# A transposed triangular inverse taken by VectorE in 32x32 blocks, and norm sums kept as columns and spread by TensorE

## The reference

```
def chunk_gated_delta(q, k, v, g, beta, s0):
    ...
    lmat = jnp.where(strict, jnp.einsum('nbhid,nbhjd->nbhij', k_beta, kb) * decay, 0.0)
    rhs = jnp.concatenate([vb * bb[..., None], k_beta * jnp.exp(gc)[..., None]], axis=-1)
    sol = lax.linalg.triangular_solve(lmat + jnp.eye(c, dtype=F32), rhs, left_side=True,
                                      lower=True, unit_diagonal=True)
    u, w = sol[..., :dv], sol[..., dv:]
    ...

def gated_deltanet(h, conv_buf, s0, w_qkv, w_conv, w_ab, dt_bias, a_log, w_g, o_norm_g, w_out):
    ...
    o, s_new = chunk_gated_delta(q, k, v, g, beta, s0)
    gate = jax.nn.silu(h @ w_g).reshape(bsz, t, GDN_HEADS, GDN_DV)
    o = rmsnorm(o, o_norm_g) * gate
    return o.reshape(bsz, t, GDN_HEADS * GDN_DV) @ w_out, new_buf, s_new
```

## Time and profile before

| | us |
|---|---|
| median of 3 runs | 1561.23 (1558.59 to 1562.16) |
| the profiled execution, its own time | 1560.17 |
| its span, first to last instruction | 1558.4 |
| heads, from 1113 to 1285 of the span | 172 |

### The profile page before, as it was taken

One profiled execution on the slowest core, in us unless ns is written; L12 is line 12 of the kernel. 1 busy time (PEld: TensorE's weight loads), 2 busy tenths in 40 slices (PEclk: granted clock), 3 DMA queues, 4 the chain that ended last, 5 costly groups with the idle time before them and its releaser, 6 DMA issues.

```text
span 1558.4 us, 32581 instructions
## 1 busy us (share of the span) xinstructions
PE 1524.9 (98%) x10378; PEld 1486.8 (95%) x10378; DVE 803.6 (52%) x1791; ACT 734.4 (47%) x1406; POOL 1082.0 (69%) x1040
## 2 busy tenths in 40 slices
PE   9999999999999999999999999999899999999998
PEld 8999999998999999888999999999888889999997
DVE  4555554017555313996555521666668766555401
ACT  6654444445444435566544433557544424444432
POOL 5568887764777678986777767766645656767674
PEclk9999999999999999999999999999999999999999
DMA  6344444552444655322656445544411215444453
GB/s 238 122 131 150 157 148 152 149 147 93 152 159 140 164 148 160 101 63 87 168 152 166 138 137 142 192 129 141 129 60 66 83 69 183 150 158 141 125 151 111
DMA packets 88110, 212.49 MB, mean 136 GB/s; under 512 B 25600, under 2 KB 33312, under 8 KB 88032
## 3 DMA queue, kind: packets, MB, share of 16 engines
q1 hardware_dynamic: 88032, 211.49, 44.1%
HBM read 201.80 MB, written 9.66 MB: 136 GB/s over the span
## 4 chain that ended last, share of the span: by engine, by line
PE 92%; DVE 4%; issue 1%; ACT 1%; POOL 1%; DMA 1%; DVEq 0%; SPq 0%; POOLq 0%; ACTq 0%
PE bank L887 26%; PE bank L889 26%; PE bank L888 26%; PE bank L1125 2%; PE bank L1264 2%; PE bank L1286 1%; PE bank L1275 1%; PE bank L1324 1%; PE bank L1178 1%; DMA fst<-in_d_st 1%; POOL M L715 0%; DVE bank L2247 0%; PE bank L1354 0%; PE bank L1306 0%; DVE ssq L1939 0%
## 5 line engine op out<-in xcount | busy, mean ns | idle before, releaser
L609 POOL TENSOR_TENSOR wlo<-raw,whi 128x512 fp32r<-128x512 f32 (+3 forms) x398 | 458.0, 1151 | 378.8 <-ACT whi L1417 341.2
L887 PE MATMUL bank<-Gh,whi 128*128 128x320 f32 x1912 | 597.3, 312 | 3.1 <-DVE M L2229 1.9
L889 PE MATMUL bank<-Gh,wlo 128*128 128x320 f32 x1912 | 591.9, 310 | 0.0
L888 PE MATMUL bank<-Gl,whi 128*128 128x320 f32 x1912 | 591.8, 310 | 0.0
L611 POOL TENSOR_TENSOR wlo<-raw,whi 128x512 fp32r<-128x512 f32 (+3 forms) x398 | 478.6, 1203 | 0.0
L1417 ACT ACTIVATE whi<-raw 128x1024 fp32r<-128x1024 f32 (+3 forms) x400 | 374.8, 954 | 53.2 <-PE bank L889 38.9
L887 PEld LDWEIGHTS bank<-Gh,whi 128*128 128x128 f32 x1912 | 360.0, 188 | 5.4 <-DVE M L2229 2.2
L888 PEld LDWEIGHTS bank<-Gl,whi 128*128 128x128 f32 x1912 | 359.9, 188 | 1.1
L889 PEld LDWEIGHTS bank<-Gh,wlo 128*128 128x128 f32 x1912 | 359.8, 188 | 0.0
L887 PE MATMUL bank<-Hh,whi 128*128 128x320 f32 x912 | 283.9, 311 | 4.0 <-DVE Hl L2188 2.5
L889 PE MATMUL bank<-Hh,wlo 128*128 128x320 f32 x912 | 282.2, 309 | 0.0
(11 more groups left out here) (388 smaller groups left out, 1844.9 us busy)
## 6 DMA issues: line engine op xcount, KB each, us to landing
raw<-in_f_up SPq DMA_DIRECT2D x176, 512.0 KB, 3.4
raw<-in_f_down SPq DMA_DIRECT2D x64, 384.0 KB, 3.2
raw<-in_f_down SPq DMA_DIRECT2D x64, 320.0 KB, 3.2
raw<-in_c_pw SPq DMA_DIRECT2D x24, 512.0 KB, 3.7
raw<-in_a_in SPq DMA_DIRECT2D x16, 512.0 KB, 3.9
raw<-in_d_qk SPq DMA_DIRECT2D x16, 512.0 KB, 3.6
raw<-in_d_vg SPq DMA_DIRECT2D x16, 512.0 KB, 3.6
raw<-in_a_out SPq DMA_DIRECT2D x8, 512.0 KB, 3.5
```

The source lines that it names most:

```text
L609: pool.tensor_tensor(wlo[k][:, 0:half], raw[k][:, 0:half], whi[k][:, 0:half].bitcast(F32), ALU.subtract).then_inc(half_ready, 1)
L887: nc.tensor.matmul(dst, wh, h, start=start and n == 0, stop=False)
L888: nc.tensor.matmul(dst, wh, lo, start=False, stop=False)
L889: ins = nc.tensor.matmul(dst, wl, h, start=False, stop=stop and end and n == len(tiles) - 1)
```

## The change

The third product of levels 0 to 3 goes. Up to there the inverse has no entry outside diagonal blocks of 32, so DVE transposes `Tm` into `TT` in blocks of 32x32. Level 4 keeps its product under a new name. The sum of squares becomes three columns (tokens along the partitions): `sq` is the weight of the product and one column of ones is what moves. ACT takes the root of 3 columns, DVE inverts the 6 of both heads at once, and PE spreads them over the partitions with a product of the broadcast column and the identity; `head_scale` reads the result in PSUM. In pairs 1 to 3 this is done within levels 2 and 3 of the inverse (for the pair before), for the last pair behind the first unit of `d_out`.

```
 def gdn_pair(b):                                  # PE
-    def change_turned(lev, x):
-        ...
-        for c in range(3 if lev < 2 else 2):
+    def last_change_turned(x):
+        pe.wait_ge(b_ready, b * 10 + (9 + x))
+        pe.wait_ge(inv_ready, b * 10 + (7 + x))
+        pe.wait_ge(kv_scaled, b * 2 + (x + 1))
+        for c in range(2):
             ins = nc.tensor.matmul(T(bank[4 * x + 2], c), T(Bm[x], c), T(TT[x], c), start=True, stop=True)
         ins.then_inc(tb_done, 1)
     for lev in range(5):
-        below(lev, 0)
-        if lev > 0:
-            change_turned(lev - 1, 1)
-        below(lev, 1)
-        if lev < 4:
-            change(lev, 0)
-        change_turned(lev, 0)
-        if lev < 4:
-            change(lev, 1)
-    change_turned(4, 1)
+        for x in range(2):
+            below(lev, x)
+        if lev in (2, 3) and not isinstance(b, int):
+            pe.wait_ge(rinv_ready, b * 1)
+            pe.wait_ge(qt_ready, b * 2 + (lev - 1))
+            spread(lev - 2, bank[4 * (lev - 2) + 1])
+        for x in range(2):
+            if lev < 4:
+                change(lev, x)
+            else:
+                last_change_turned(x)
...
+                        if not isinstance(b, int):
+                            pe.wait_ge(h_mid, b * 2 + (htile(3, False) + x - 1))
                         nc.tensor.matmul(T(bb, 0), T(TT[x], 0), T(vp[x], 0), start=True, stop=True).then_inc(u_done, 1)
...
-                        nc.tensor.matmul(bank[4 * x + 2][:, 0:NT], ones[:, :], sq[x][:, 0:NT], start=True, stop=True)\
-                            .then_inc(osum_done, 1)
+                        for i, (first, _, _) in enumerate(TOKENS):
+                            ins = nc.tensor.matmul(bank[4 * x + 2][:, TW + i:TW + i + 1], sq[x][:, first:first + P], ones[:, 0:1],
+                                                   start=True, stop=True)
+                        ins.then_inc(osum_done, 1)
...
+def spread(x, dst):                               # PE
+    for i, (first, a, z) in enumerate(TOKENS):
+        ins = nc.tensor.matmul(dst[:, a:z], rinv[x][:, i:i + 1].to_broadcast([P, P]),
+                               ident[:, a - first:z - first], start=True, stop=True)
+    ins.then_inc(spread_done, 1)
...
                 for m in range(4):                # PE, d_out
                     pe.wait_ge(ss_ready, 7 + m // 2)
                     unit(u0 + m, m, Hh, Hl, d_out_banks[m][:, 0:NT], range(6), ready=(h_ready, h0), end=False)
+                    if m == 0:
+                        pe.wait_ge(rinv_ready, 4)
+                        for x in range(2):
+                            pe.wait_ge(s_ready, 31 + x)
+                            spread(x, bank[4 * x + 2])
...
-                        nc.scalar.activation(sq[x][:, 0:NT], bank[4 * x + 2][:, 0:NT], ACT.Sqrt, scale=1.0 / P,
+                        nc.scalar.activation(rinv[x], bank[4 * x + 2][:, TW:TW + 3], ACT.Sqrt, scale=1.0 / P,
...
-def head_invert(h, x, i):                         # DVE
-    dve.wait_ge(osd_ready, h + (x + 1))
-    q = sq[x][:, NT // 4 * i:NT // 4 * (i + 1)]
-    S.mark(vec.reciprocal(q, q))
+def head_inverse(n):
+    dve.wait_ge(osd_ready, n)
+    vec.reciprocal(dc[:, 2:8], dc[:, 2:8]).then_inc(rinv_ready, 1)
...
 for lev in range(5):                              # DVE
-    for x in range(2):
-        if lev < 4:
-            ... Tm[x] -= bank[4 * x + 3]
-        if later and x == 1 and lev < 4:
-            head_invert(b * 2 - 2, lev // 2, 2 * (lev % 2))
-        ... TT[x] -= bank[4 * x + 2]
-    if later and 2 <= lev < 4:
-        head_invert(b * 2 - 2, lev - 2, 1)
+    if lev < 4:
+        for x in range(2):
+            ... Tm[x] -= bank[4 * x + 3]
+        for x in range(2):
+            dve.wait_ge(tm_ready, b * 8 + (2 * lev + x + 1))
+            vec.transpose(TT[x][:, 0:w], Tm[x][:, 0:w]).then_inc(inv_ready, 1)
+    else:
+        ... TT[x] -= bank[4 * x + 2]                for both x
+    if later and lev in (2, 3):
+        head_scale(b * 2 - 2, lev - 2, bank[4 * (lev - 2) + 1])
...
                         if c == 0 and later:
-                            head_invert(b * 2 - 2, 0, 3)
-                            head_invert(b * 2 - 2, 1, 3)
-                            head_scale(b * 2 - 2, 0)
-                            head_scale(b * 2 - 2, 1)
```

More of the change, by code:

```diff
@@ L373, in trunk_kernel @@
         scr_n = nc.dram_tensor("scr_n", [2 * HEADS, NT], F32).ap()
+        rinv = [dc[:, 2 + 3 * x:5 + 3 * x] for x in range(2)]
+        TOKENS = ((0, 0, P), (P, P, 2 * P), (NT - P, 2 * P, NT))
         GDN_STORED = 18 + 1 + 2 * HEADS
@@ L391, in trunk_kernel @@
         LN_READY, GT_READY, SQRT_READY, RW_READY_A, COLS_READY = 3, 4, 7, 9, 10
-        PAIR_STEPS = 14
+        PAIR_STEPS = 6
         block = ctx.enter_context(nc.Block())
@@ L672, in scaled_keys @@
                     if not (isinstance(b, int) and b == 0):
[L673 removed]
+                        pool.wait_ge(tb_done, b * 2 + (x - 1))
                     pool.wait_ge(k_ready, b * 2 + (x + 1))
@@ L1389, in _ @@
                     if m >= 6:
-                        pe.wait_ge(osd_ready, 7)
                         pe.wait_ge(og_ready, 7)
+                        pe.wait_ge(h_mid, h0 + 7)
                     unit(u0 + m, m % 4, Hh, Hl, d_out_banks[m][:, 0:NT], range(KT))
@@ L2421, in differences, with head_scale @@
                     ins.then_inc(diff_ready if dst is dec else diffi_ready, 1)
-                def head_invert(h, x, i):
-                    dve.wait_ge(osd_ready, h + (x + 1))
-                    q = sq[x][:, NT // 4 * i:NT // 4 * (i + 1)]
-                    S.mark(vec.reciprocal(q, q))
-                def head_scale(h, x):
-                    S.wait()
+                def head_inverse(n):
+                    dve.wait_ge(osd_ready, n)
+                    vec.reciprocal(dc[:, 2:8], dc[:, 2:8]).then_inc(rinv_ready, 1)
+                def head_scale(h, x, src):
+                    dve.wait_ge(spread_done, h + (x + 1))
                     dve.wait_ge(og_ready, h + (x + 1))
-                    vec.tensor_tensor(hbuf[x][:, :], hbuf[x][:, :], sq[x][:, 0:NT], ALU.mult).then_inc(h_mid, 1)
+                    vec.tensor_tensor(hbuf[x][:, :], hbuf[x][:, :], src[:, 0:NT], ALU.mult).then_inc(h_mid, 1)
                 S.wait()
@@ L2465, in gdn_pair @@
                                 S.mark(ins)
+                    if later:
+                        head_inverse(b * 2)
                     for lev in range(5):
                         w = (3 if lev < 2 else 2) * P
-                        for x in range(2):
-                            if lev < 4:
+                        if lev < 4:
+                            for x in range(2):
                                 dve.wait_ge(bt_done, b * 8 + (2 * lev + x + 1))
@@ L2472, in gdn_pair @@
                                     .then_inc(tm_ready, 1)
[L2473 to L2479 removed]
+                            for x in range(2):
+                                dve.wait_ge(tm_ready, b * 8 + (2 * lev + x + 1))
+                                vec.transpose(TT[x][:, 0:w], Tm[x][:, 0:w]).then_inc(inv_ready, 1)
+                        else:
+                            for x in range(2):
+                                dve.wait_ge(tb_done, b * 2 + (x + 1))
+                                vec.tensor_tensor(TT[x][:, 0:w], TT[x][:, 0:w], bank[4 * x + 2][:, 0:w], ALU.subtract)\
+                                    .then_inc(inv_ready, 1)
+                        if later and lev in (2, 3):
+                            head_scale(b * 2 - 2, lev - 2, bank[4 * (lev - 2) + 1])
                         if lev == 4 and not last:
@@ L2509, in gdn_pair @@
                                                          op0=ALU.mult, op1=ALU.add).then_inc(s_ready, 1)
-                        if c == 0 and later:
-                            head_invert(b * 2 - 2, 0, 3)
-                            head_invert(b * 2 - 2, 1, 3)
-                            head_scale(b * 2 - 2, 0)
-                            head_scale(b * 2 - 2, 1)
                         if c in (0, 2):
@@ L2541, in _ @@
                 gdn_pair(3, True)
-                for i in range(4):
-                    for x in range(2):
-                        head_invert(6, x, i)
+                head_inverse(8)
                 for x in range(2):
-                    head_scale(6, x)
+                    head_scale(6, x, bank[4 * x + 2])
                 out_phase("d_out", 3, plain_add, d_out_banks)
```

9 lines of the change are left out of this document (1 added, 8 removed).

## The result

The changed kernel is slower: 1565.52 us in the median of 20 runs (1560.35 to 1573.15) against 1560.48 us for the kernel before (20 runs, 1558.59 to 1563.81). The ratio is 1.0032, with a 95% interval of 1.0023 to 1.0042. 1554.2 us was forecast, with a range up to 1561.5. The new runs scatter over 13 us where the old ones scatter over 5, and their mean granted clock goes with it: 0.987 or 0.988 in the three fastest at 1560 to 1561 us, 0.980 in the two slowest at 1572 and 1573. The profiled execution (1560.89 us, span 1558.8, clock 0.987) is the third fastest.

What follows compares the result with a forecast made beforehand. PE, busy in 98% of the span, was taken as the bound; 2.0 + 3.75 + 1.9 - 1.3 = 6.35 us won gave 1553.8 us profiled, forecast as a 1554.2 us median, range 1549 to 1561.5.

Steps and rivals of the forecast that it cites:

- part 1: Inverse, levels 0 to 3: dropping the third product wins 2.0 us in pair 0; 1.25 us carried for each later pair.
- The two spreads of a pair: Levels 2 and 3 of the inverse, pairs 1 to 3: 0.2 and 0.1 us lost against the kernel before.
- Part 3: Behind chunk 0: DVE's scalings go, so PE's waits for the late copy vanish; 1.9 us won in all.
- the sum: Whole kernel: 2.0 + 3.75 + 1.9 - 1.3 = 6.35 us won.
- the value taken: DVE's transposes in the inverse: 0.50 us for 384 columns and 0.37 us for 256.
- The rival of the lock: Inverse, levels 0 and 1: DVE's transposes and POOL's masks lock each other out, 9.6 us lost, 1563.4 us; chance 0.09.
- Three idle times: PE's waits behind chunk 0: 1.5 us, with 0.1 us for each restart, 1.9 us in all.
- ACT's two roots: Norm: ACT's root is shorter by nearly 1 us, but PE isn't waiting for it.
- part 4: Sums: twelve one-column matmuls take 1.3 us against 1.34, no change; two spreads behind the last pair lose 1.3 us.
- The clock rival: Thinner inverse: PE's clock falls to 1.2 GHz, 1.7 us a fall; four more give 1560.5, six 1564 us; chance 0.07.
- Its sign: Pairs 1 and 2: a granted clock no longer at 1.00 would show the forecast wrong.
- Parts 2 and 4: Spreads within levels 2 and 3 lose 0.2 and 0.1 us a pair; the two within `d_out` lose 1.3 us.

Runs made afterwards that it cites:

- e1: The kernel before with the transposed inverse alone, without the spread and with all of the norm as before: 1554.02 us, ratio 0.9973.
- e9: The kernel before with the sums' four matmuls of 320 columns a pair replaced by twelve unused one-column products: 1568.48 us, ratio 1.0050.
- e3: The changed kernel with each of the sum's products moving 128 columns of ones in place of one: 1557.32 us, ratio 0.9979.
- e8: e1 with unused products of 128 columns as fillers in levels 0 to 3 of the inverse, 16 a pair: 1557.26 us, ratio 0.9983.
- e5: e1 with each head's eight sample products moving 128 to 16 columns in place of 16, plus an extra DVE addition: 1553.62 us, ratio 0.9954.
- e6: The changed kernel with sums of 128 columns, spreads queued behind the changes, and the wider sample products of e5: 1555.53 us, ratio 0.9961.
- e7: The kernel before with only the wider sample products of e5: 1563.03 us, ratio 1.0004.
- e10: e5 with the wide sums replaced by the narrow, unused one-column sums: 1562.61 us, ratio 1.0018.

## Why the prediction was wrong

**What held.** The gain of part 1 for pairs 1 to 3 was 0.9 us each (15.87 to 14.97) where 1.25 was carried, and pair 0's, 2.0 forecast, was 3.7 in the traces (L1264 at 1123.7 to L1306 at 1141.2 before, 13.7 us now). Part of that is a fall in the old trace: e1, with a fall at the same place, took 15.1 us, so that 2.3 are the gain. The two spreads of a pair cost 1.1 us (levels 2 and 3 against those of pair 0), where the sum had 0.95. Part 3 gave 0.75 us in pair 1 (17.93 to 17.17) against 0.63. By the lines, at an equal clock, the changed kernel has 5.2 us less than the kernel before, where the sum said 6.35. The transposes of the changed kernel, lines by form, in the columns of the earlier trace rows:

```profile
L2494 DVE STREAM_TRANSPOSE Hl_spare<-M 128x384 f32<-128x384 f32 x16 | 8.2, 553 | 0.0
...
L2494 DVE STREAM_TRANSPOSE Hl_spare<-M 128x256 f32<-128x256 f32 x16 | 6.1, 419 | 0.0
```

They took 553 and 419 ns, 0.05 us above the value taken and far below the 0.65 us at which they would have counted. The estimate of 0.58 us for 384 columns from the Trainium skill's "VectorE: DVE Perf Modes" ("The three transpose paths") was the closer one. The rival of the lock falls: of the sixteen of 384 columns those of level 0 stood beside POOL's masks and those of level 1 didn't, and two of them took 1.03 us in both places. By the rule of the Trainium skill's "SBUF — State Buffer" ("Who interferes with whom") a lock concerns two SBUF inputs or a two-port mode. The trace agrees with the first (1352 against 485 ns), and it shows no such lock for the transpose.

**Slips in the sum.** Three idle times, 1.5 us together, and three restarts of 0.1 are 1.8 us, not 1.9; ACT's two roots became 0.53 us shorter (264 against 527 ns each), not nearly 1, and nothing waits for them; and 1553.8 us with the 1.06 us that the median lies higher is 1554.9, not 1554.2. None of this decides anything.

**The step that failed is part 4, the sums.** It priced the twelve one-column products by their issue time, 1.3 us, found that equal to the four wide ones, and wrote no change, with bounds of 0.3 us over all four pairs. Their own time is nearly that: 1.59 against 1.34 us behind pair 0, 0.25 us more. But in place of 1280 columns that move in this stretch there are 12, and TensorE's clock fell behind it. e9 shows that the sums alone cost 8.9 us in the kernel before; e3 shows that the same number of instructions with 128 columns each are 8.2 us quicker. The clock rival had the right mechanism and the price of a short fall (1.7 us; 7.00 us at 0.53 in e9 are 3.3 us of full clock, and 11.00 us at 0.53 in e8 are 5.2), but put it into the thinner inverse and gave it a chance of 0.07. Its sign, a clock below 1.00 in pairs 1 and 2, came: 0.69 in the set-up of pair 2. It argued from pair 2's idle times that idle time didn't bring a fall, without asking which products move few columns. Yet the samples' 16 matmuls of 16 columns and the fall in the chunk stage of pair 3 stood there to be seen, and in the timeline of the kernel before they stand next to each other:

```profile
1273.14 1.91 PE L1324 MATMUL bank<-Hl_spare,M 128*128 128x16 f32 x16
...
1275.34 0.63 PE L1342 MATMUL bank<-Hh_spare,Hl_spare 128*128 128x128 f32 x2
```

The two matmuls of L1342 take 0.63 us there and 0.44 at full clock.

**The inverse and the falls.** e1 shows that the thinner inverse alone leaves most runs at the old clock. A quarter of them lie lower, at 0.984 to 0.986; no trace of such a run of e1 was taken. In e5, with wider samples, none of six lies there, and fillers inside the inverse (e8) didn't remove the low runs. The long falls in the traces of e3 and e8 begin at or just behind sample products. This speaks for the samples as their place, but it isn't shown: six runs are few, and with wider samples e6 and e7 still have falls of 4 us, in the first `below` of a pair and in sums of 320 columns, and e5 a long one. So the one-column sums bring more and longer falls (e9, e10 and e3), but few columns aren't the only thing ahead of one. What else brings them, and why none of the 69 runs of the kernel before in these rounds lies below 0.989, stays open.

**Parts 2 and 4 in the tail.** Norm and spreads cost even at equal clock: by the lines e3 is 3.3 us above e1 there. The six spreads on the chain (1.1 us a pair) and the two within `d_out` (12 matmuls, 1.3 us at full clock) cost more than part 3 saves. So the lowest medians are those of the inverse without the new norm: e1 with 1554.02 and e5 with 1553.62 us, both clearly below the kernel before, though the intervals of e3 and e6 overlap theirs.

## What to carry to other kernels

Taking a product off a full engine is worth what the next chain leaves: here 0.9 us of 4.5 in each pair from 1 on, and the chain could be added up from rows within 0.2 us a level. When a rewrite turns wide products into narrow ones at the same count and duration, the price isn't in their own time but in what follows: look at the granted clock behind the narrow products that are already there, and widen the moving side if it costs nothing. Judge such a change by many runs with their clocks, since one profile can lie at the lucky end.

## What the runs showed of the hardware

- Twelve fp32 matmul instructions with 128 rows of weights take 1.59 us with one moving column and 1.60 us with 128. With one column the mean granted clock was 0.9842, with 128 it was 0.9899.
- PE's busy time doesn't tell it: 7.00 of 7.00 us at 0.53 of the clock (e9). The Trainium skill's "TensorE: Matmul & The Clock Gate" ("What's actually happening") says that the clock gate goes by how busy the PE has been of late. By that rule the twelve products should count like the twelve of 128 columns, which are as long; the runs don't agree with it where busy is read as the profile's busy time.
- Half clock lasted about 4, 7 or 11 us in the traces of this case (1154.5 to 1158 and 1195.5 to 1202.5 in the changed kernel, 1146 to 1156.5 in e3). At half clock a head's 16 sample matmuls took 3.5 us in place of 1.9, and the low clock went on through them, as the timeline of PE in e3, chunk stages of pair 0, shows:

```profile
1143.28 1.91 PE L1335 MATMUL bank<-Hl_spare,M 128*128 128x16 f32 x16
...
1148.77 3.54 PE L1335 MATMUL bank<-Hl_spare,M 128*128 128x16 f32 x16
1152.14 0.67 PE L1336 MATMUL bank<-Hl_spare,Hh_spare 128*128 128x64 f32 x2
```

- DVE's transpose of 32x32 fp32 blocks took 553 ns for 384 columns and 419 ns for 256, and POOL's masks beside it, of 256 columns, took 0.73 us (0.75 in the kernel before).
